# The root mean square of the S5 mixer's output: one number per token, spread by ones times diagonals

## The reference

```python
def rmsnorm(x, g):
    xf = x.astype(F32)
    y = xf * lax.rsqrt(jnp.mean(xf * xf, axis=-1, keepdims=True) + EPS)
    return (y * g.astype(F32)).astype(x.dtype)

def s5_mixer(u, ..., w_glu, b_glu, norm_g):
    ...
    y = jax.nn.gelu(y.reshape(bsz, s, D_C))
    out = y * jax.nn.sigmoid(y @ w_glu.astype(F32) + b_glu.astype(F32))
    return rmsnorm(out, norm_g).astype(u.dtype)
```

## Time and profile before

| | us |
|---|---|
| median of three runs | 3302.71 |
| lowest, highest | 3301.82, 3305.93 |
| profiled execution | 3302.13 |
| its span | 3300.0 |
| `state_space`, first to last instruction | 1003.6 to 1161.4 |

### The profile page before, as it was taken

One profiled execution on the slowest core, in us unless ns is written; L12 is line 12 of the kernel. 1 busy time (PEld: TensorE's weight loads), 2 busy tenths in 40 slices (PEclk: granted clock), 3 DMA queues, 4 the chain that ended last, 5 costly groups with the idle time before them and its releaser, 6 DMA issues. The chain is left out here.

```text
span 3300.0 us, 51424 instructions
## 1 busy us (share of the span) xinstructions
PE 3097.1 (94%) x20672; PEld 2522.9 (76%) x20672; DVE 2163.1 (66%) x3314; ACT 1337.0 (41%) x2133; POOL 493.3 (15%) x650
## 2 busy tenths in 40 slices
PE   8999999699998889989999889999899999999998
PEld 6777777588887668767888768888688887877776
DVE  6666575667656557544444476777777767777776
ACT  5646656445541322113333243333433333444443
POOL 4333333566750001100000000000000000000000
PEclk9999999899999989999999999999899999999999
DMA  6263655212110264330112333233323334766764
GB/s 215 91 212 97 209 154 168 94 60 80 62 50 8 75 232 153 121 121 32 64 57 70 109 109 109 102 110 140 109 102 112 112 112 138 250 205 214 238 206 143
DMA packets 200073, 416.21 MB, mean 126 GB/s; under 512 B 15280, under 2 KB 99504, under 8 KB 193456
## 3 DMA queue, kind: packets, MB, share of 16 engines
q1 hardware_dynamic: 199856, 413.18, 38.0%
HBM read 295.66 MB, written 117.46 MB: 125 GB/s over the span
## 5 line engine op out<-in xcount | busy, mean ns | idle before, releaser
L2921 PE MATMUL ffn_ps<-ffn_t_p,ffn_w_p 128*128 128x512 f32 x2640 | 619.8, 394 | 2.5 <-DVE ffn_w_p L3094 2.5
L2921 PEld LDWEIGHTS ffn_ps<-ffn_t_p,ffn_w_p 128*128 128x128 f32 x2640 | 496.5, 188 | 118.8 <-DVE ffn_w_p L3094 3.6
L2936 PE MATMUL ffn_ps<-ffn_t_p_parts 128*128 128x512 f32 x1416 | 332.3, 393 | 11.2 <-DVE ffn_t_p_parts L3236 7.0
L2936 PEld LDWEIGHTS ffn_ps<-ffn_t_p_parts 128*128 128x128 f32 x1416 | 264.8, 189 | 74.3 <-DVE ffn_t_p_parts L3236 14.6
L485 PE MATMUL proj<-hn_high,w_high 128*128 128x512 f32 x672 | 278.3, 421 | 17.5 <-ACT t_ag L554 14.6
L485 PE MATMUL proj<-hn_low,w_high 128*128 128x512 f32 x672 | 267.5, 402 | 5.9 <-DVE hn_low L693 4.4
L397 POOL TENSOR_TENSOR w_low<-w_ring,w_high 128x1024 fp32r<-128x1024 f32 x84 | 211.0, 2515 | 367.5 <-ACT w_high L530 367.5
L485 PE MATMUL proj<-hn_high,w_low 128*128 128x512 f32 x672 | 261.5, 396 | 0.0
L2947 ACT ACTIVATE ffn_w_p<-ffn_w_p_sums 128x512 fp32r<-128x512 f32 x132 | 83.5, 633 | 342.9 <-DVE ffn_w_p_sums L3115 342.7
L485 PEld LDWEIGHTS proj<-hn_high,w_high 128*128 128x128 f32 x672 | 128.6, 192 | 54.5 <-ACT t_ag L554 16.3
L2936 PE MATMUL ffn_ps<-ffn_t_p 128*128 128x512 f32 x696 | 164.0, 391 | 3.3 <-DVE ffn_t_p_sums L3317 2.6
(11 more groups left out here) (496 smaller groups left out, 6489.6 us busy)
## 6 DMA issues: line engine op xcount, KB each, us to landing
ffn_ring<-in_w_up SPq DMA_DIRECT2D x44, 1024.0 KB, 5.4
ffn_ring<-in_w_down SPq DMA_DIRECT2D x88, 512.0 KB, 5.5
w_ring<-in_w_feat SPq DMA_DIRECT2D x84, 512.0 KB, 3.7
ffn_ring<-scratch_values SPq DMA_DIRECT2D x88, 257.0 KB, 4.5
scratch_gates<-ffn_gate SPq DMA_DIRECT2D x44, 512.0 KB, 2.6
ffn_ring<-scratch_gates SPq DMA_DIRECT2D x88, 256.0 KB, 3.9
scan_in<-scratch_scan SPq DMA_DIRECT2D x16, 896.0 KB, 4.5
scratch_values<-ffn_raw SPq DMA_DIRECT2D x22, 513.0 KB, 3.7
```

The lines of the kernel that those rows point to most:

```text
L2921: mm = pe.matmul(bank(name, s), w_part(name, a)[:, k * P:(k + 1) * P], t_part(name, b)[:, k * TB:(k + 1) * TB], start=k == a == b == 0, st ...
L2936: mm = pe.matmul(ps[:, DOWN_BANKS[2 * t + c]], down_part(n, x)[:, HID + t * TC:HID + (t + 1) * TC], down_part(n, y)[:, c * DH:(c + 1) * DH ...
```

## The change

The squares become the weights and one column of the all-ones matrix the moving operand, so that a matmul gives the sums of 128 tokens as one column, one token in each partition: 32 matmuls of one column in the place of eight of 512. Mean, root and reciprocal are then of 128 x 4 for each block. To bring the 512 numbers of a block back along the free dimension and into all partitions, VectorE multiplies the identity by each column (16 diagonals of 128 x 128) and TensorE multiplies the all-ones matrix by each diagonal (16 matmuls of 128 columns) into bank `b`. The final products read that bank. VectorE's work is split into three loops over the blocks: means, then reciprocals with diagonals, then final products. TensorE does the 16 new matmuls (`n_wide`) between the sums of squares and the key/value tiles. `s5_diag` takes the place and the size of `s5_inv`, and `rms` lies in a buffer that is free by then.

```diff
-        inv = sb("s5_inv", [P, SEQ])
+        diag = sb("s5_diag", [P, SEQ // P, P])
...
-        m_sq = mi[:, 0, 0:MT]
+        m_sq, rms = mi[:, 0, 0:MT], mr[:, 0, 0:SEQ // P]
...
+        n_diag, n_wide = sig("n_diag", NB), sig("n_wide", NB)
...
-                act.activation(inv[:, b * TB:(b + 1) * TB], inv[:, b * TB:(b + 1) * TB], ACT.Sqrt).then_inc(n_root.sem, 1)
+                act.activation(rms[:, b * CB:(b + 1) * CB], rms[:, b * CB:(b + 1) * CB], ACT.Sqrt).then_inc(n_root.sem, 1)
...
             for b in range(NB):
-                at = slice(b * TB, (b + 1) * TB)
                 dve.wait_ge(*n_done.at(0, b))
-                ts(inv[:, at], ps[:, b], 1.0 / (G2 * P), EPS, MUL, ADD).then_inc(n_out.sem, 1)
+                ts(rms[:, b * CB:(b + 1) * CB], ps[:, b, 0:CB], 1.0 / (G2 * P), EPS, MUL, ADD).then_inc(n_out.sem, 1)
+            for b in range(NB):
+                at = slice(b * CB, (b + 1) * CB)
+                dve.wait_ge(*n_root.at(0, b))
+                me.done(dve.reciprocal(rms[:, at], rms[:, at]))
+                for j in range(b * CB, (b + 1) * CB):
+                    last = ts(diag[:, j], ident, rms[:, j:j + 1], None, MUL)
+                last.then_inc(n_diag.sem, 1)
             for b in range(NB):
                 at = slice(b * TB, (b + 1) * TB)
-                dve.wait_ge(*n_root.at(0, b))
-                me.done(dve.reciprocal(inv[:, at], inv[:, at]))
+                dve.wait_ge(*n_wide.at(0, b))
                 dve.wait_ge(*sq_ready.at(0, G2 * b + 1))
                 for t in range(G2):
-                    last = stt(yt[:, t, at], yt[:, t, at], col("s5_norm", t), inv[:, at], MUL, MUL)
+                    last = stt(yt[:, t, at], yt[:, t, at], col("s5_norm", t), ps[:, b], MUL, MUL)
                 last.then_inc(yc_ready.sem, 1)
...
                 pe.wait_ge(*sq_ready.at(0, G2 * b + 1))
-                for k in range(G2):
-                    mm = pe.matmul(ps[:, b], ones, sq[:, k, b * TB:(b + 1) * TB], start=k == 0, stop=k == G2 - 1)
+                for j in range(CB):
+                    for k in range(G2):
+                        mm = pe.matmul(ps[:, b, j:j + 1], sq[:, k, (b * CB + j) * P:(b * CB + j + 1) * P], ones[:, 0:1],
+                                       start=k == 0, stop=k == G2 - 1)
                 mm.then_inc(n_done.sem, 1)
+            for b in range(NB):
+                pe.wait_ge(*n_diag.at(0, b))
+                for j in range(CB):
+                    mm = pe.matmul(ps[:, b, j * P:(j + 1) * P], ones, diag[:, b * CB + j], start=True, stop=True)
+                mm.then_inc(n_wide.sem, 1)
             pe.wait_ge(*mn_ready.at(0))
```

## The result

The changed kernel takes 3310.03 us (median of 20 runs, 3303.39 to 3312.84) against 3304.49 (20 runs, 3300.39 to 3309.39). The ratio is 1.0015, interval 1.0009 to 1.0022: slower by about 5 us, 3 to 7.3 us by the interval. The forecast was +3.5 us; it lies in this interval, and so does rival B's +6.6 to +7.3. By the absolute times the forecast of 3306 fared worse: 3310.03 is only 0.5 us inside the upper end of the stated range (3310.5), and just past the 3309.3 to 3310 of rival B. About 1.8 us of that distance is the kernel before, whose median was 3302.71 in the forecast's three runs and is 3304.49 here. So the time alone doesn't tell the forecast from B; the profile does.

What follows compares the result with a forecast made beforehand. VectorE's reciprocals and products, then stores, bound the S5 tail; TensorE is busy 94% overall. 7.5 us of VectorE's delay won, 11 us of TensorE's lost: +3.5 us on 3302.13, plus 0.6 for the median, gives 3306; range 3299.5 to 3310.5.

Steps and rivals of the forecast that it cites:

- rival B: S5 tail: clock stays low through the spread and into the key/value tiles; +6.6 to +7.3 us, 3309.3 to 3310; chance 0.16.
- the room: S5 tail: faster VectorE work can win at most 7.5 us before TensorE with ScalarE sets the end.
- One-column matmuls: Sums of squares on TensorE: weight load paces each record, 0.107 us at full clock, 0.214 us at half.
- C: Sums of squares: one-column matmuls are cheap, 0.053 us or less a record; 3298 to 3300; chance 0.06.
- The clock under the sums: TensorE's clock falls at about 1128.4 and stays at half through the one-column sums; last sum at 1139.6, against 1135.8.
- A: Sums of squares: the clock comes back at 1131.8 as before, despite one-column matmuls; -2.0 us, 3300.7; chance 0.15.
- The spread: 16 matmuls of ones times diagonals before the key/value tiles: 5.6 us, 4.3 at half clock; tiles begin 11 us late.
- What is last: End of S5: key/value tiles and ScalarE's last copy, not stores (4 us of cover); next function at 1165.6, +3.5 us.
- so this is worth nothing: `mix_out`'s first key/value tile, 5.38 us at half clock, may run at full clock; no gain, ScalarE's first square awaits a load.
- The added instructions in the streams I cost at nothing: Instruction streams of the engines: the change's added instructions cost no time.
- if `mix_out`'s first waits change in length: Start of `mix_out`, sign of being wrong: the sum fails if the first waits there change in length.
- one later spell: TensorE after later pauses: a 3.3 us low-clock spell may fall otherwise, up to 1.7 us to either side.

Runs made afterwards that it cites:

- e5: Kernel before without the four 128x512 reciprocals, the output scaled by the root; ratio 0.9965 (five runs), tail of S5 31.2 us.
- e2: Changed kernel with each of the 32 matmuls of the sums streaming 128 columns of ones instead of one; ratio 0.9994, tail 37.0 us.
- e10: Kernel before with 160 waits on a semaphore long reached, in TensorE's program ahead of the gate's product; tail 37.3 us.
- e1: Changed kernel again without an edit, for a second profile; ratio 1.0013, tail 42.4 us.
- e8: Kernel before again, for a second profile of `mix_out`'s first steps; tail 39.0 us, first steps 10.8 us.
- e11: Kernel before with 24 waits on a semaphore long reached, in VectorE's program ahead of the four evictions; tail 39.1 us.
- e7: Changed kernel with three idle 512-column matmuls behind `mix_out`'s first key/value tile; tail 42.4 us, first steps 12.0 us.

## Why the prediction was right, and where a term was not

**VectorE and the room.** 39.0 to 31.2 without the reciprocals: 7.8 us, 7.5 in the text; 0.2 of the 0.3 us between them is the clock that didn't fall in e5.

**One-column matmuls.** 0.213 us a record at half clock by the evictions, 0.214 in the text. C falls. At nearly full clock (0.95) 12 records take 1.36 us, 0.11 each. (The Trainium skill, TensorE: Matmul & The Clock Gate, section Back-to-back issue gap, gives its 25 ns for 1 to 64 columns as the gap of a matmul taken by itself, and says that in a stream of weight loads and matmuls both set the spacing; here, where each matmul loads its own weights, 0.11 us was measured. The 107 ns for a load of 128 columns, section LDWEIGHTS (loading the stationary operand), agrees with it.)

**The clock under the sums.** It falls at about 1131.7, 1.2 us into them (1.4 in the text), and stays at 0.50; the last sum is there 12.7 us after the start of the first, 12.6 in the text. A falls. e2 shows that it is the single column that keeps it down, and not the weight loads alone. That it would fall at all was taken from the one profile of before, and there is luck in it: e5 and e10 have the same pause and no fall.

**The spread.** 5.7 us from its start to the first tile (5.6), the clock back 4.4 us into it (4.3), the tiles 19.7 us after the sums' start (19.7), and not touched by the low clock. B falls.

**What is last.** The engines, as the queue's wait shows; the stores were covered. The tail is +3.3 us, forecast +3.5. A small slip had no effect: the text lets VectorE's last product follow the last spread, at about 1148.1, though eight products of 0.67 us that begin behind the last diagonal alone take until 1149.4 by its own numbers; moved by the 3.4 us ahead of the tail, the measured end is 1149.1.

**What failed: "so this is worth nothing".** That was the step on `mix_out`'s first tile. I saw that a faster tile would end in a wait for the load and stopped there; the tile was faster (3.69 us for 5.38). The wait is a pause of 2.8 us, and behind it the clock fell in both profiles: 4.8 to 5.0 us for a tile of 3.6, and the first steps 1.8 us longer. **And "The added instructions in the streams I cost at nothing"**: 1.1 us, by a fetch that now falls into the loads. Together the first steps are 2.9 to 3.1 us longer. The text had named this as a sign of being wrong ("if `mix_out`'s first waits change in length"), and it came true. Not all of it stays. Weight loads of the output product (min/median/max ns, first and last start), before and after:

```profile
L2048 PEld LDWEIGHTS ps_w<-w_out_high,mix_high x256: 187/188/334, 1195.7 to 1390.8; 128*128 128x128 f32 x128
```

```profile
L2061 PEld LDWEIGHTS ps_w<-w_out_high,mix_high x256: 187/188/190, 1205.5 to 1399.0; 128*128 128x128 f32 x128
```

None is over 190 ns after (and in e1), while before some are 334 (329 in e8): a low-clock spell at the product's start that the changed kernel doesn't have in its two profiles. All of `mix_out` is 1.3 us longer (234.8 and 235.0 against 236.3 and 236.1). With the tail's 3.3 this makes 4.6 us, and 5.0 were measured (3.0 to 7.3). The 3.3 us and the 3 us in the first steps repeat; the 1.3 us are not shown clear of chance. e11, whose computation and whose first steps are those of before, has 235.7 us of `mix_out`, e2 with first steps of 11.9 has the longest, 236.9, and from `mix_out`'s end to the end of the kernel both profiles of the changed one are shorter by about 1 us (1901.8 and 1902.0 against 1903.0 and 1902.9). So the mechanism in the tail was right; the term for what lies behind was put at nothing without a reason, and its net size is open.

Left open as well: how the spells of low clock fall in `mix_out`; their times were read, not set by an edit. The text allowed for one later spell, up to 1.7 us to either side; that size fits the 1.8 us of the pause, but not its cause. If the kernel before has its 37.3 us tail in a part of its executions, as in e10, the loss against it is 5.1 us there, which would also help to explain the 5.0 us measured; no run tells how large that part is. And the text's "about 0.2%" for what can be told from no change was too wide: 20 runs told 0.15%.

## What to carry to other kernels

When work is moved into the stream of the engine that is late next, cost it in that engine's stream and at the clock that it will get: a matmul with one moving column cost as much as one with 128 at the same clock, as the weight loads filled the time of both, and under it the clock stayed at half where it came back after 3.4 us with 128. A step that ends the earlier only to wait is not free either: on TensorE look at what runs behind the pause, and take a second profile, since a pause of the same length had the low clock behind it in one and not in the other. And where a chain on one engine is shortened, put what it hands to another engine behind that engine's independent work, but only once the clock is kept: alone the move won 0.4 us, with the clock 1.8.

## What the runs showed of the hardware

- TensorE at half clock for 17 us with its matmul and weight-load records at 2.0 us of each 2 us: the busy share of the records doesn't tell its clock. 64 records took 12.7 us with one column and 9.0 us with 128.
- The same pause of 2.27 us ahead of the sums was followed by the low clock in eleven profiles and not in two (e5, e10): sums of 8.8 or 7.1 us, and with them tails of 39.0 or 37.3 us of the kernel before.
- With an instruction fetch of one packet (0.02 MB) on its own queue 2 us behind `mix_out`'s first instruction, the loads then under way landed 0.9 us later (4.6 to 5.5 us) and their reader started 1.1 us later (4.9 to 5.9). Its place moved with the number of instructions ahead of it in TensorE's program: 80 more put it elsewhere, 160 more put it there.
- The same kernel's profiles differ by 3 us in where its tail begins (1126.5, 1123.5), while the tail repeats to 0.1 us where the clock falls alike (42.4 in after, e1 and e7; 39.0 to 39.1 in before, e8 and e11).
